# A modulation vector moved from 192 TensorE products to GpSimd accumulation with twelve strip products

## What is computed

```python
cond = jax.nn.silu(c)                        # 1 x 1024
mod = cond @ mod_w[l] + mod_b[l]             # 1024 x 6144 weights, 24 MB
sh1, sc1, g1, sh2, sc2, g2 = split(mod, 6)
h = rmsnorm(x, norm1_g) * (1 + sc1) + sh1    # second network only
...
x = x + g1 * mix
h = rmsnorm(x, norm2_g) * (1 + sc2) + sh2
x = x + g2 * moe(h)                          # 32 experts
```

## Time and profile before

| what | before |
|---|---|
| median of 3 runs (lowest to highest) | 1403.77 us (1403.49 to 1404.3) |
| span of the profiled execution | 1399.9 us |
| TensorE busy | 1186.8 us, 85% |
| VectorE busy | 593.1 us, 42% |
| ScalarE busy | 436.0 us, 31% |
| GpSimd busy | 22.6 us, 2% |

### The profile page before, as it was taken

One profiled execution on the slowest core, in us unless ns is written; L12 is line 12 of the kernel. 1 busy time (PEld: TensorE's weight loads), 2 busy tenths in 40 slices (PEclk: granted clock), 3 DMA queues, 4 the chain that ended last, 5 costly groups with the idle time before them and its releaser, 6 DMA issues.

```text
span 1399.9 us, 19232 instructions
## 1 busy us (share of the span) xinstructions
PE 1186.8 (85%) x8218; PEld 868.8 (62%) x8218; DVE 593.1 (42%) x971; ACT 436.0 (31%) x689; POOL 22.6 (2%) x45
## 2 busy tenths in 40 slices
PE   6999989999999999999999999898664745647477
PEld 6998756699887787589988777654321312213132
DVE  5688413576643675366644548833100101001011
ACT  4653320344433585354433431543010000000001
POOL 4000000000000000000000000000000000000000
PEclk9999999999999999999999999999787868878699
DMA  8352669355554555145554624777999999999997
GB/s 274 132 205 97 211 214 360 128 181 181 189 207 174 204 180 180 61 162 185 185 190 151 228 88 152 270 297 299 426 427 430 427 428 428 429 427 431 427 422 281
DMA packets 103052, 362.98 MB, mean 259 GB/s; under 512 B 7844, under 2 KB 13296, under 8 KB 92096
## 3 DMA queue, kind: packets, MB, share of 16 engines
q1 hardware_dynamic: 100736, 357.64, 66.2%
q0 software_dynamic: 2096, 4.17, 1.1%
q10 hardware_dynamic: 144, 0.07, 0.0%
HBM read 360.81 MB, written 1.05 MB: 258 GB/s over the span
## 4 chain that ended last, share of the span: by engine, by line
PE 61%; DMA 22%; DVE 5%; issue 2%; ACT 2%; SPq 1%; DVEq 0%; ACTq 0%
PE bank L935 33%; DMA arena<-in_exp_w 20%; PE bank L637 8%; PE bank L1049 3%; PE bank L907 3%; PE bank L917 2%; PE bank L1242 2%; PE bank L874 2%; PE bank L1589 1%; DMA ring<-in_exp_w 1%; SPq L2843 1%; PE bank L1259 1%; PE bank L1273 1%; PE bank L1287 1%; PE bank L1456 1%
## 5 line engine op out<-in xcount | busy, mean ns | idle before, releaser
L637 PE MATMUL bank<-arena 128*32 128x512 f32 x880 | 187.2, 676 | 69.6 <-DMA arena<-in_exp_w 69.6
L1740 DVE TENSOR_TENSOR low_w<-ring,split_high 128x2048 fp32r<-128x2048 f32 x84 | 189.6, 2288 | 104.3 <-ACT split_high L2438 104.2
L935 PE MATMUL bank<-turned_high,low_w 128*128 128x256 f32 x720 | 204.6, 284 | 0.0
L2438 ACT ACTIVATE split_high<-ring 128x2048 fp32r<-128x2048 f32 x84 | 157.8, 1917 | 136.5 <-DMA ring<-in_w_down 67.7
L637 PE MATMUL bank<-ring,arena 128*32 128x512 f32 x528 | 98.1, 721 | 82.0 <-DMA arena<-in_exp_w 80.9
L935 PE MATMUL bank<-turned_high,split_high 128*128 128x256 f32 x512 | 145.9, 285 | 3.0 <-DVE turned_low L1755 3.0
L935 PE MATMUL bank<-turned_low,split_high 128*128 128x256 f32 x512 | 144.9, 283 | 0.0
L935 PEld LDWEIGHTS bank<-turned_high,low_w 128*128 128x128 f32 x720 | 139.1, 193 | 0.0
L637 PEld LDWEIGHTS bank<-arena 128*32 128x32 f32 x880 | 47.7, 123 | 128.8 <-issue 128.6
L789 DVE TENSOR_TENSOR arena<-arena,bank 128x512 f32<-128x512 f32 x8 | 5.5, 687 | 271.1 <-PE bank L637 243.2
L637 PEld LDWEIGHTS bank<-ring,arena 128*32 128x32 f32 x528 | 27.2, 129 | 148.5 <-issue 147.4
(11 more groups left out here) (469 smaller groups left out, 1924.2 us busy)
## 6 DMA issues: line engine op xcount, KB each, us to landing
arena<-in_exp_w SPq DMA_DIRECT2D x51, 2048.0 KB, 23.6
ring<-in_exp_w SPq DMA_DIRECT2D x33, 2048.0 KB, 19.1
ring<-in_w_up SPq DMA_DIRECT2D x16, 2048.0 KB, 9.0
ring<-in_w_down SPq DMA_DIRECT2D x16, 2048.0 KB, 7.8
ring<-in_mod_w SPq DMA_DIRECT2D x12, 2048.0 KB, 8.5
arena<-in_exp_w SPq DMA_DIRECT2D x33, 512.0 KB, 13.8
ring<-in_w_in_ar SPq DMA_DIRECT2D x6, 2048.0 KB, 8.2
ring<-in_w_qkv SPq DMA_DIRECT2D x6, 2048.0 KB, 7.9
```

Of the source, the lines that this page charges most:

```text
L637: last = nc.tensor.matmul(mb[bank][strip(e), :], act[:, k, strip(e)], w[e][:, k, cols], start=(k == 0), stop=(k == n_k - 1), skip_group_ch ...
L935: last = mm(dst, *pair, start=(start and i == 0), stop=(stop and i == 2))
L1740: v.tensor_tensor(low_of(name, s), half_of(slot(name), name, s), high_of(name, s).bitcast(F32), ALU.subtract).then_inc(sem("split_low"), 1)
L2438: nc.scalar.activation(high_of(name, s), half_of(slot(name), name, s), ACT.Copy)\
```

## The change

`mod` leaves the ring's list. GpSimd loads `mod_w` itself in 48 pieces of 128x1024 (512 KB) into two buffers in `spare`. Chunk c (of six) is the sum over the eight blocks k of cond[k] times piece: a `tensor_scalar` (multiply by a value for each partition) and, for k > 0, a `tensor_tensor` add into an accumulator, 48 of the one and 42 of the other. Accumulators alternate between a part of `spare` and `big_row`. The first chunk starts when VectorE has raised `tilded`, the signal that the RWKV inputs are scaled. Chunk c + 2 waits until TensorE has read chunk c.

TensorE now only sums over partitions: `mod_part(c)`, two products with a strip that has one column of ones. Parts 0 and 1 stand in the two scan steps between "sa" and "y"; parts 2, 3 and 4 behind units 1, 4 and 7 of the first up phase; part 5 behind the first half of `down`. VectorE takes each part into `mod_sum` (`take_mod`, 64x512). GpSimd's later loads (`big_row`, the gains, `p`) follow behind its loop.

```diff
-            def modulation(*units_):
-                for c in units_:
-                    w = blocks(weights(pe, "mod", c), KC)
-                    for k in range(KC):
-                        strip = slice(STRIP * (k % 4), STRIP * (k % 4 + 1))
-                        at = MOD_UNITS - 1 - c
-                        last = mm(mod_bank.ap[strip, :], cond3[:, k, at:at + STRIP], w[:, k, :],
...
+            def mod_part(c):
+
+                pe.wait_ge(sem("mod_step"), KC * (c + 1))
+                bank = banks.take(pe, "mod_part", c)
+                for n in range(2):
+                    u = 2 * c + n
+                    at = MOD_UNITS - 1 - u
+                    last = mm(bank.ap[STRIP * (u % 4):STRIP * (u % 4 + 1), :], one_strip[:, at:at + STRIP],
+                              mod_acc[c % 2][:, n * 512:(n + 1) * 512], start=True, stop=True, skip_group_check=True)
+                last.then_inc(bank.full, 1)
...
+            load_mod(0)
+            load_mod(1)
+            pool.wait_ge(sem("cond_ready"), 1)
+            pool.wait_ge(sem("tilded"), 1)
+            for i in range(KC * MOD_CHUNKS):
+                c, k = i // KC, i % KC
+                acc, piece = mod_acc[c % 2], mod_piece[i % 2]
+                if k == 0 and c >= 2:
+                    banks.read(pool, "mod_part", c - 2)
+                pool.wait_ge(sem(f"mod_landed{i % 2}"), 16 * (i // 2 + 1))
+                scaled = acc if k == 0 else piece
+                last = nc.gpsimd.tensor_scalar(scaled, piece, cond[:, k:k + 1], None, ALU.mult)
+                if k > 0:
+                    last.then_inc(sem("mod_scaled"), 1)
+                    pool.wait_ge(sem("mod_scaled"), i - c)
+                    last = nc.gpsimd.tensor_tensor(acc, acc, piece, ALU.add)
+                last.then_inc(sem("mod_step"), 1)
+                pool.wait_ge(sem("mod_step"), i + 1)
+                if i + 2 < KC * MOD_CHUNKS:
+                    load_mod(i + 2)
+            banks.read(pool, "mod_part", MOD_CHUNKS - 1)
```

More of the change, by code:

```diff
@@ L44 @@
 MOD_UNITS = 12
+MOD_CHUNKS = MOD_UNITS // 2
 MOD_ROWS = [4, 5, 10, 11]
@@ L268, in build @@
         mod_sum = spare[:, 0:512]
-        cond_wide = STRIP + MOD_UNITS - 1
-        cond_strips = spare[:, 512:512 + KC * cond_wide]
+        one_wide = STRIP + MOD_UNITS - 1
+        one_strip, cond = spare[:, 512:512 + one_wide], spare[:, 576:576 + KC]
+        mod_piece = [spare[:, 2048:3072], spare[:, 3072:4096]]
+        mod_acc = [spare[:, 1024:2048], big_row_t[:, :]]
         big_row = big_row_t[:, :]
@@ L1278, in _ @@
                     last.then_inc(bank.full, 1)
-                modulation(n)
                 for g in range(4):
@@ L1330, in _ @@
                 last.then_inc(bank.full, 1)
-                modulation(7 + 3 * t)
+                mod_part(t)
                 banks.wait_read(pe, "sa", t)
@@ L1352, in _ @@
                     from_state(pair, t, 1)
-                modulation(8 + 3 * t)
                 if t == 0:
@@ L1388, in feed_forward @@
                     split_features(("up", l, c), ("up", l, c))
+                    if l == 0 and c in (1, 4, 7):
+                        mod_part(2 + c // 3)
                 for n in range(2):
@@ L1394, in feed_forward @@
                         split_down(l, n, kb, pair)
+                    if l == 0 and n == 0:
+                        mod_part(MOD_CHUNKS - 1)
                 for t in range(NT):
@@ L1405, in feed_forward @@
                 if l == 0:
-                    banks.wait_read(pe, "mod")
+                    banks.wait_read(pe, "mod_part", MOD_CHUNKS - 1)
                     bank = banks.take(pe, "mod_columns")
@@ L1770, in _ @@
             v.memset(vec_rows, 0.0).then_inc(sem("vec_zero"), 1)
-            v.memset(cond_strips[:, :], 0.0).then_inc(sem("cond_zero"), 1)
+            step(v.memset(one_strip, 0.0))
+            step(v.memset(one_strip[:, MOD_UNITS - 1:MOD_UNITS], 1.0))
             for i in range(2):
@@ L2020, in take_halves, with take_mod @@
                                   blocks(bank.ap[:, 0:S], 4)).then_inc(bank.freed, 1)
+            def take_mod(c):
+                bank = banks.read(dve, "mod_part", c)
+                own = mod_rows(c)
+                if c < 2:
+                    step(v.tensor_copy(mod_sum[own], bank.ap[own, :]))
+                else:
+                    step(v.tensor_tensor(mod_sum[own], mod_sum[own], bank.ap[own, :], ALU.add))
+                v.memset(next(flag), 0.0).then_inc(bank.freed, 1)
             for t in range(NT):
@@ L2024, in _ @@
                 evacuate(sa_sb, "sa", t)
+                take_mod(t)
                 if t == 0:
@@ L2080, in feed_forward @@
                             .then_inc(sem("act_ready"), 1)
+                    if l == 0 and c in (1, 4, 7):
+                        take_mod(2 + c // 3)
                 for n in range(2):
@@ L2084, in feed_forward @@
                     add_to_x("down", l, ns=(n,), scale=rstd2)
+                    if l == 0 and n == 0:
+                        take_mod(MOD_CHUNKS - 1)
                 turned_lows(("x_gate", l), range(KC // 2))
```

41 lines of the change are left out of this document (16 added, 25 removed).

## The result

| what | before | after |
|---|---|---|
| median of 4 runs (lowest to highest) | 1403.63 us (1401.34 to 1404.3) | 1463.14 us (1460.12 to 1464.4) |
| ratio, 95% interval | | 1.0418 [1.0392, 1.0444] |
| span of the profiled execution | 1399.9 us | 1462.6 us |
| GpSimd busy | 22.6 us | 322.9 us |
| VectorE busy | 593.1 us | 649.6 us |

The prediction was 1390 us, with a range to 1420. The change costs 59 us, and the sign was wrong.

A forecast was written before the change was run, and what follows sets the result against it. TensorE was taken to bound the kernel (85% busy, 61% of the chain of waits). 1403.8 - 17.75 (products out) - 4 (stalls) + 3.8 (parts) + 4 (turns) = 1389.9, said as 1390 us; own range 1378 to 1400, overall to 1420.

The forecast's parts named there:

- GpSimd's price: GpSimd's loop: multiply 1.3 us, add 2.3, a piece 4.4 us of work (3.3 to 5.7), 4.9 with loads.
- It holds by 6 us: Part 1 in the scan: its 16 pieces ready at 206 us, TensorE there at about 212.
- later deadlines: Parts 2 to 5, feed-forward net: more air for GpSimd, 7 us a piece, then 8.6 for the fifth chunk.
- Turns with GpSimd: VectorE and GpSimd alternating on a shared read path: 0 to 20 us added, 4 taken.
- the critical places: y normalisation and gate, and first two splits: nine VectorE waits of up to 2.3 us, 20 us at most.
- rival 1: Turn-taking in the up phase delays TensorE 13 to 26 us, 8 to 13 ahead: 1407 to 1425, middle 1416; chance 0.35.
- operations stretched: Sign of rival 1 in the trace: GpSimd operations lasting beyond 2.3 us.
- Rival 2: Slow loads make pieces 6.4 us, chunk 1 ends at 230, TensorE waits 18 us at part 1: 1408; chance 0.09.
- The TensorE sum: Inversion, scan and following turns: products removed gain 17.75 us, stalls 4 more, parts add 3.8.
- stalls: Long units and "issue" waits, mainly in the inversion, may go with less load traffic: 0 to 7 us, 4 taken.
- The four parts: Four parts in the feed-forward net, where TensorE has no gap: 4 x 0.95 = 3.8 us added.
- Moved on GpSimd's queue: Loads of `p`, gains and `big_row` behind the loop stay hidden: loop ends about 395, `p` wanted at 447.7, 50 us spare.

The follow-up runs named there:

- no_gpsimd_const: The changed kernel without GpSimd's loads and arithmetic for the modulation, TensorE's parts summing a constant (modulation left out): 1390.98 us, ratio 0.9920.
- free_early_p: Against `free_parts`, the loads of the gains and `p` moved from behind GpSimd's loop to its piece 20: 1414.32 us, ratio 1.0069.
- late_loads: The changed kernel with GpSimd's first two loads issued only once the condition vector is ready: 1457.39 us, ratio 1.0388.
- free_parts: Against `no_gpsimd_const`, GpSimd's whole loop put back, first loads late, nobody waiting for its sums: 1423.58 us, ratio 1.0140.
- quiet_window: Kernel before, with GpSimd making four of twelve modulation units ahead of the turns and feed-forward net, eight staying on TensorE: 1399.75 us, ratio 0.9984.
- scan_fillers: Against `no_gpsimd_const`, six groups of eight short products put back into the scan, their sums thrown away: 1389.27 us, ratio 0.9913.
- no_gpsimd: The changed kernel without GpSimd's loop, parts summing accumulators cleared once; experts took another path: 2409 us, ratio 1.717; feed-forward net ended at 429.6 us.
- the small kernel: Separate kernel, not an edit: eight operations in a row on GpSimd, VectorE and both; VectorE's add with one PSUM input 5.74 us alone and together.

## Why the prediction was wrong

Summed from the ratios (0.001 = 1.4 us), from the kernel before to the one after:

| step | from the runs | us |
|---|---|---|
| TensorE's products out, parts in | no_gpsimd_const | -11.2 |
| GpSimd's loop beside the others (turns, traffic) | free_early_p | +20.9 |
| parts wait for GpSimd | late_loads | +44.8 |
| first loads beside `w_in` | after | +4.2 |
| sum | | +58.7 |

Each row is the difference of two ratios that follow each other, so the sum closes by itself; what the runs show is the sizes. The last two rows carry some 6 us of uncertainty each way.

**The step that failed first: GpSimd's price, and with it "It holds by 6 us".** I took 1.3 us for the multiply from VectorE's row and bounded it between 1.22 and twice that, 2.44. It is 2.85 us, outside the bounds. I reasoned that one input less must be cheaper than the add; on GpSimd the multiply with one input is the dearer of the two (add 2.35, assumed 2.3). With 0.6 for issuing and 0.4 of signals a piece is 6.2 us, not 4.9 or the upper 5.7. Part 1 was ready at 230.8 instead of 206, with TensorE there at 217.5; in the 97.5 us of these 16 pieces GpSimd sat idle for a load for only 1.0, so the lateness is its own price. My later deadlines left 7 to 8.6 us a piece, but with turns a piece took 7.3 us there (25 from 277.8 to 459.2), and the lead was lost already. Even without turns 42 x 6.2 and 6 x 3.8 (the pieces without an add), 283 us from 133, end at 416, past part 5's 395: I never multiplied the whole loop out against its last deadline at a slow price.

**Turns with GpSimd, taken as 4.** The runs give 20.9 us, with the loads' share in it. The 4 were for the critical places, where 5.0 were measured; the up phase, which the forecast took at nothing, cost 11.0. The mechanism of rival 1 was right, down to both of VectorE's kinds of operation and to "operations stretched"; 13 to 26 in the up phase was 11.0 in `free_parts`, less than its lower end, and 5.0 in the critical places ahead against 8 to 13. The chance was too small. The Trainium skill (SBUF — State Buffer, "Who interferes with whom") stated the rule outright. Against it I had only "need not be under way" and "if VectorE keeps the path", and no row for either, though GpSimd was to work without a pause, 3.6 of every 4.9 us.

**Rivals 1 and 2 as alternatives.** I gave each a time of its own. They belong together: turns make pieces longer, longer pieces miss deadlines, and the wait for a deadline is larger than the turn that caused it. Both were true at once; 1416 and 1408 were the sums of one each. Rival 2's 6.4 us a piece and its end of chunk 1 at 230 came out (6.2 and 230.8), but by luck: it had them from slow landings, and the loads landed in 4.3 us (median), quicker than any figure I had used.

**The TensorE sum.** At the start of the up phase it said -21.75, or -17.95 with the four parts and no turns at the end of `down`; measured -19.3 and -14.5. The total is fair, its places are not. The inversion: 11.1 from units and 4 (0 to 7) from stalls against 19.5. If the units gave their 11.1, as the four of `quiet_window` gave theirs, the stalls were worth about 8, past the upper end; that the waits for "issue" are a price of traffic is shown by the two runs with loads and without. The 3.27 us unit that I counted among the stalls is something else: it stands in the scan at a granted clock of 0.54, with no wait in it. The scan: from its start to the up phase 6.65 was expected, and the stretch became 0.3 us longer (scan -1.0, the turns behind it +1.4). I read each unit's exposed copy and never the granted clock, which the units themselves kept up; `scan_fillers` shows it. In `no_gpsimd`, with the clock at 0.81, the scan alone gave 4.9. The four parts: 3.8 expected, 4.7 measured (3.4 for three in the up phase, 1.3 for one in the down phase). The lower end of the range was mis-added too: all stalls gone and no turns is 1403.8 - 17.75 - 7 + 3.8 = 1383, not 1378.

**Moved on GpSimd's queue.** "Hidden, 50 us to spare" failed with the price: `p` would have cost 10.0 us if the loop alone had been late. In the kernel after it doesn't show, since TensorE was later still.

**The first loads.** I counted 24 MB leaving the ring and nothing for 1 MB arriving at 24 us beside `w_in`: 4.2 us by the ratios, 5.7 by the trace.

## What to carry to other kernels

Price a helper engine per piece from a measured instruction of that very form, multiply the whole loop out against its last deadline at the slow end, and count it as two costs that feed each other: what it takes from its neighbour, and what it is then late by. A GpSimd loop that reads SBUF belongs where VectorE has little to do: four units there, in the broadcast form, gained 0.16% (interval 0.03 to 0.29%), and twelve across a busy stretch lost 4.2%. (By the small kernel it may also run beside a VectorE that reads PSUM; no whole kernel here tried that.) Products that look like fillers can be what keeps TensorE's clock up: before removing them from a stretch of short batches, read the granted clock with and without them, in more than one execution.

## What was unexpected in the hardware

- GpSimd, 128x1024 float32 (an eighth of eight in a row): multiply by a value for each partition 2.92 us, by a constant 2.84, the same multiply as an operation with two inputs, one of them broadcast, 1.96, add 2.41, copy 1.09.
- Eight VectorE adds take 10.04 us alone, 26.35 beside GpSimd's add, 13.17 beside GpSimd's multiply. The slower instruction alone is the milder neighbour.
- Six groups of products, 11.1 us of work, made the scan only 2.8 us longer: the granted clock was 0.70 without them and 0.94 with them. In two other executions without them it was 0.81, and the scan 3.8 us shorter.
- TensorE's "issue" stalls in the inversion were 6.6 us at 241 GB/s of loads and under 1 us without.
